# Token rows picked by index: 64 tokens on two partition halves, or 96 tokens on 96 partitions

## What is computed

```python
gate = softmax(top_s)                                   # 8 heads x 16 per token
u = take(expert_u, eidx)                                # row of 1024 for each picked expert
act = gelu(einsum('thkd,td->thk', u, xb))
v = take(expert_v, eidx)
out = einsum('thk,thkd->td', gate * act, v)
```

## Time and profile before

| | us |
|---|---|
| median of 3 runs | 2746.68 (2738.3 to 2747.53) |
| profiled execution, its own time | 2742.25 |
| its span, first to last instruction | 2740.9 |
| TensorE busy | 2560.6 (93%) |
| VectorE busy | 1730.9 (63%) |
| ScalarE busy | 1015.2 (37%) |
| GpSimd busy | 381.0 (14%) |
| matmuls of 448 columns, up and down | 6144 |

### The profile page before, as it was taken

The page is one execution under the profiler, slowest core; times in us unless marked ns, Lnnn a source line. Parts: engine busy times, 40 slices in busy tenths (PEclk is TensorE's granted clock), DMA queues, the critical chain, the costliest instruction groups (busy, mean ns, idle before and its releaser), DMA issues.

```text
span 2740.9 us, 33410 instructions
## 1 busy us (share of the span) xinstructions
PE 2560.6 (93%) x12530; PEld 2093.6 (76%) x12530; DVE 1730.9 (63%) x3522; ACT 1015.2 (37%) x1687; POOL 381.0 (14%) x256
## 2 busy tenths in 40 slices
PE   7989999999999999999999999899877899999997
PEld 5768988988888888999999997678644476645555
DVE  7898867766676665766777645553467645255564
ACT  3332333343333332333333333432256523244443
POOL 4010444440000001212222000200000020000001
PEclk9999999999999999999999999999899999999999
DMA  6546444446566569998999753111100012100001
GB/s 237 181 170 231 144 144 144 144 151 215 199 212 220 200 216 336 317 300 278 317 318 303 242 204 117 56 52 62 38 1 1 1 63 76 64 18 18 18 1 62
DMA packets 148415, 415.91 MB, mean 152 GB/s; under 512 B 13664, under 2 KB 75232, under 8 KB 145568
## 3 DMA queue, kind: packets, MB, share of 16 engines
q1 hardware_dynamic: 100896, 317.31, 33.2%
q0 software_dynamic: 18432, 67.12, 7.4%
q10 hardware_dynamic: 28928, 29.36, 3.4%
HBM read 352.62 MB, written 60.82 MB: 151 GB/s over the span
## 4 chain that ended last, share of the span: by engine, by line
PE 83%; DVE 9%; ACT 4%; issue 4%; POOL 1%; DMA 0%; ACTq 0%; DVEq 0%
PE psum L542 8%; PE psum L543 8%; PE psum L544 8%; PE psum L411 7%; PE psum L413 7%; PE psum L412 7%; PE psum L403 5%; PE psum L405 5%; PE psum L404 5%; PE psum L515 4%; PE psum L827 2%; PE psum L429 2%; DVE small L1669 2%; PE psum L847 2%; PE psum L696 1%
## 5 line engine op out<-in xcount | busy, mean ns | idle before, releaser
L1332 DVE TENSOR_TENSOR weights_low<-arena,weights_high 128x1024 fp32r<-128x1024 f32 x290 | 364.1, 1256 | 517.2 <-ACT weights_high L904 516.6
L904 ACT ACTIVATE weights_high<-arena 128x1024 fp32r<-128x1024 f32 x355 | 374.4, 1055 | 560.5 <-PE psum L544 412.5
L411 PE MATMUL psum<-x_high,weights_high 128*128 128x448 f32 x1024 | 380.4, 371 | 7.6 <-POOL weights_low L1862 7.6
L542 PE MATMUL psum<-hidden_high,weights_high 128*128 128x448 f32 x1024 | 375.9, 367 | 6.8 <-issue 6.8
L543 PE MATMUL psum<-hidden_low,weights_high 128*128 128x448 f32 x1024 | 375.0, 366 | 0.0
L544 PE MATMUL psum<-hidden_high,weights_low 128*128 128x448 f32 x1024 | 375.0, 366 | 0.0
L413 PE MATMUL psum<-x_high,weights_low 128*128 128x448 f32 x1024 | 374.1, 365 | 0.0
L412 PE MATMUL psum<-x_low,weights_high 128*128 128x448 f32 x1024 | 374.0, 365 | 0.0
L403 PE MATMUL psum<-x_high,weights_high 128*128 128x512 f32 (+1 forms) x696 | 277.8, 399 | 24.3 <-DVE weights_low L1332 19.4
L404 PE MATMUL psum<-x_low,weights_high 128*128 128x512 f32 (+1 forms) x696 | 272.6, 392 | 0.0
L405 PE MATMUL psum<-x_high,weights_low 128*128 128x512 f32 (+1 forms) x696 | 272.6, 392 | 0.0
(11 more groups left out here) (239 smaller groups left out, 3976.9 us busy)
## 6 DMA issues: line engine op xcount, KB each, us to landing
arena<-in_stream SPq DMA_DIRECT2D x227, 512.0 KB
arena<-in_v_rows SPq DMA_DIRECT2D x128, 512.0 KB
hidden<-arena SPq DMA_DIRECT2D x128, 224.0 KB, 2.5
router<-arena SPq DMA_DIRECT2D x14, 2048.0 KB, 8.3
arena<-hidden SPq DMA_DIRECT2D x128, 224.0 KB, 4.9
arena<-router ACTq DMA_DIRECT2D x16, 1792.0 KB
arena<-in_ada_w SPq DMA_DIRECT2D x48, 512.0 KB, 3.4
arena<-in_pair_w SPq DMA_DIRECT2D x8, 576.0 KB, 3.8
```

What stands on the lines that cost most here:

```text
L411: PE.matmul(bank[b][:, 0:N], wh[u % 2][:, k, :], xh[:, k, PICKED:T], start=k == 0, stop=False)
L542: PE.matmul(out, wh[w][:, n, :], hh[:, r, :], start=e == 0, stop=False)
L904: ACT.activation(wh[u % 2], slots[u % RING], AF.Copy).then_inc(*tick("weights_high", u))
L1332: DVE.tensor_tensor(wl[u % 2], slots[u % RING], wh[u % 2].bitcast(F32), ALU.subtract).then_inc(*tick("weights", u))
```

## The change

`PICKED` goes from 64 to 96, one token per partition on 96 partitions, all 128 entries of a token there; so N is 416, there are 104 quads and 13 stages, and 256 rows are gathered (128 of each table, 96 partitions each) instead of 128. Rows of both tables come in turn: an `expert_v` row of entry n follows 12 entries behind its `expert_u` row, gelu and the product with the gates are done in groups of 8 entries, and there is one sum. The moves between partitions and `twice` go. VectorE uses one row in each of up steps 6 to 56, two in each of 57 to 63, and 191 rows spread over down steps 0 to 123. `weigh_hidden` goes from VectorE to GpSimd, two steps ahead, in one list with the gathers.

```diff
-PICKED = 64
+PICKED = 96
 N = T - PICKED
-PICKS = PICKED * ENTRIES // P
+GROUP = 8
+ROW_LAG = 12
...
+    ROWS = []
+    for n in range(ENTRIES + ROW_LAG):
+        ROWS += [("u", n)] * (n < ENTRIES) + [("v", n - ROW_LAG)] * (n >= ROW_LAG)
+    ROW_STEPS = [("up", n) for n in range(1, KEYS - UNDER_ROUTER)] + [("down", e) for e in range(KEYS)]
+    ROWS_AT = {step: [] for step in ROW_STEPS}
+    LAST_ROWS = KEYS - 4
+    early = len(range(6, 57)) + 2 * len(range(57, 64))
+    for j in range(early):
+        ROWS_AT["up", 6 + j if j < 51 else 57 + (j - 51) // 2].append(j)
+    for e in range(LAST_ROWS):
+        rest = len(ROWS) - early
+        ROWS_AT["down", e] = list(range(early + e * rest // LAST_ROWS, early + (e + 1) * rest // LAST_ROWS))
...
+        def gelu_rows(step):
+            for g in GELU_AT.get(step, []):
+                part = row_act[:, g * GROUP:(g + 1) * GROUP]
+                ACT.wait_ge(*at("row_used", ROWS.index(("u", (g + 1) * GROUP - 1))))
+                ACT.activation(part, part, AF.Gelu_apprx_tanh).then_inc(*tick("row_act", g))
...
         for e in range(KEYS):
-            if e + 1 < KEYS:
-                weigh_hidden(e + 1)
             low_weights(unit("down", e) + 1)
             if e + 1 < KEYS:
                 hidden_low(e + 1)
-            use_row(("down", e))
...
+            for j in ROWS_AT["down", e]:
+                use_row(j)
...
+        def weigh_hidden(e):
...
+            POOL.wait_ge(*at(f"hidden{e % HID_RING}_in", e))
+            POOL.wait_ge(*at(f"g{e // BLOCK % 2}_in", e // BLOCK))
+            POOL.tensor_tensor(one, one, gates, ALU.mult).then_inc(*tick("weighted", e))
+
+        POOL.wait_ge(*at("chosen", 0))
+        for j in range(ROW_RING):
+            fetch_row(j)
+        for kind, n in ROW_STEPS:
+            if kind == "down":
+                for e in range(2) if n == 0 else ():
+                    weigh_hidden(e)
+                if n + 2 < KEYS:
+                    weigh_hidden(n + 2)
+            for j in ROWS_AT[kind, n]:
+                fetch_row(j + ROW_RING)
...
-        load("x_rows_moved", 0, x_rows[PICKED:P, :], x_rows[0:PICKED, :])
...
-        load("chosen_moved", 0, chosen[PICKED:P, 0:PICKS], chosen[0:PICKED, PICKS:ENTRIES])
-        load("row_gate_moved", 0, row_gate[PICKED:P, :], gate[0:PICKED, 0, PICKS:ENTRIES])
```

More of the change, by code:

```diff
@@ L337, in taken @@
         return "convolved", n - 12
[L340 to L348, removed]
+    ROWS = []
[10 more added lines that the diff above has]
+        ROWS_AT["down", e] = list(range(early + e * rest // LAST_ROWS, early + (e + 1) * rest // LAST_ROWS))
+    GELU_AT = {}
+    for at_step, step in enumerate(ROW_STEPS):
+        for j in ROWS_AT[step]:
+            if ROWS[j][0] == "u" and ROWS[j][1] % GROUP == GROUP - 1:
+                GELU_AT.setdefault(ROW_STEPS[at_step + 1], []).append(ROWS[j][1] // GROUP)
     def a_tiles(t):
@@ L548, in tensor @@
                     if n == 0:
-                        PE.wait_ge(*at("row_acc", "both"))
-                    PE.matmul(bank[n][:, 0:PICKED], row_acc[0][:, n * P:(n + 1) * P], K("twice"), start=True,
-                              stop=True).then_inc(*tick("summed_down", n))
+                        PE.wait_ge(*at("row_used", len(ROWS) - 1))
+                    PE.matmul(bank[n][:, 0:PICKED], row_acc[:, n * P:(n + 1) * P], K("ident", slice(0, PICKED))[:, 0:PICKED],
+                              start=True, stop=True).then_inc(*tick("summed_down", n))
         def embed(n):
@@ L1555, in vector @@
                 one_hots(i)
-            use_row(("up", n))
-        def weigh_hidden(e):
-            one = hidden[:, e % HID_RING, :].rearrange("p (s t) -> p s t", t=STAGE)
-            block = weight[:, e // BLOCK % 2 * STAGES:(e // BLOCK % 2 + 1) * STAGES, :]
-            gates = block.rearrange("p s (e t) -> p s e t", t=STAGE)[:, :, e % BLOCK, :]
-            DVE.wait_ge(*at(f"hidden{e % HID_RING}_in", e))
-            DVE.wait_ge(*at(f"g{e // BLOCK % 2}_in", e // BLOCK))
-            DVE.tensor_tensor(one, one, gates, ALU.mult).then_inc(*tick("weighted", e))
+            for j in ROWS_AT["up", n]:
+                use_row(j)
         def hidden_low(e):
@@ L1863, in gpsimd, with fetch_row @@
                 *tick("weights_pool", u))
[L1865 to L1867 removed]
+        def fetch_row(j):
+            if j >= len(ROWS):
+                return
             if j >= ROW_RING:
                 POOL.wait_ge(*at("row_used", j - ROW_RING))
[L1870 to L1873 removed]
+            table, entry = ROWS[j]
+            POOL.indirect_dma_start(rows[j % ROW_RING], None, d[f"{table}_rows"], bass.IndirectOffsetOnAxis(
+                ap=chosen[:, entry:entry + 1].bitcast(U32), axis=0)).then_inc(*tick(f"row{j % ROW_RING}_in", j, 16))
+        def weigh_hidden(e):
+            one = hidden[:, e % HID_RING, :].rearrange("p (s t) -> p s t", t=STAGE)
+            block = weight[:, e // BLOCK % 2 * STAGES:(e // BLOCK % 2 + 1) * STAGES, :]
+            gates = block.rearrange("p s (e t) -> p s e t", t=STAGE)[:, :, e % BLOCK, :]
+            POOL.wait_ge(*at(f"hidden{e % HID_RING}_in", e))
[12 more added lines that the diff above has]
+                fetch_row(j + ROW_RING)
         for c in range(KC - 1):
```

91 lines of the change are left out of this document (36 added, 55 removed).

## The result

The changed kernel takes 2777.97 us in the median of 4 runs (2775.98 to 2790.25), the kernel before 2747.11 beside it. The ratio is 1.0128, with a 95% interval from 1.0091 to 1.0165 (the quotient of the two medians is 1.0112). The forecast was 2684, its range 2661 to 2723. The profiled execution spans 2775.7 us, 34.8 more than the 2740.9 of before.

What follows compares the result with a forecast made beforehand. TensorE was taken to bound the first up and down stages, a four-engine ring the second up stage. Gains 17 + 11 - 1 + 35.6 = 62.6 us off 2742.25 gave 2679.6, with the median 4.4 above: 2684, range 2661 to 2723.

Steps and rivals of the forecast that it cites:

- Full DMA showed 398, so it fits at 86%: Down stage: 1.56 MB a step in 4.54 us needs 343 GB/s, within the 398 GB/s seen at full DMA.
- Rival 3: Down stage: the ring of four row buffers becomes the bound, 5.39 us a step, total 2785; chance 0.07.
- VectorE beside GpSimd: Down stage: weighing on GpSimd costs VectorE 0.85 us a step through contention, bounds 0.4 to 1.3.
- rival 1: Down stage: VectorE becomes the bound, weighing costs it 1.3 us a step, time about 2713; chance 0.20.
- 4.33 us a step, 95% of TensorE's 4.54: Down stage: VectorE's work of 3.48 us plus 0.85 for contention stays under TensorE's step.
- The first up stage: Beside the expert search: 64 units each 0.32 us shorter, less longer waits once a head; gain 17 us.
- the second: Second up stage: two-quad steps gain nothing, eight one-quad steps gain 1.6 us each, gelu loses 1.5; gain 11 us.
- the ring: Second up stage: scatter, eviction, rounding, subtraction and one-hots through four engines set a two-quad step at 7.32 us.
- Rival 2: All goes well: second up stage's ring gives way (15.4 us more), DMA adds nothing; 87 us gained, 2660; chance 0.11.
- The last seven ups and the change of stage: Between up and down stages: units gain 2.2 us, idle grows from 6.8 to about 10; net loss 1 us.

Runs made afterwards that it cites:

- e2: The changed kernel with gathers fetching rows for all 128 partitions, the last 32 unused: 2730.26 us.
- e3: The changed kernel with PICKED at 64, rows gathered to 64 partitions: 2787.12 us.
- e5: A separate kernel computing nothing, only gathers and loads: beside loads 409 GB/s with 128 partitions, 293 with 96, 260 with 64.
- e1: The changed kernel with the weighing of hidden blocks back on VectorE, 96-partition gathers kept: 2774.85 us.
- e4: The changed kernel with each gather bringing only half a row (2 KB) per partition, the other half zero: 2729.64 us.
- e6: The changed kernel with 128-partition gathers (32 unused) and the weighing back on VectorE: 2684.92 us, ratio 0.9800.
- e10: The kernel before, ScalarE rounding next weights ahead of the quads' evictions in the second up stage: that stage 405.7 to 368.5 us, kernel 1% faster.
- e11: The changed kernel, ScalarE rounding next weights ahead of the quads' evictions in the second up stage: that stage 393.1 to 341.7 us.

## Why the prediction was wrong

**The step that failed is "Full DMA showed 398, so it fits at 86%".** The 398 GB/s came from a stretch of the kernel before in which every transfer went to 128 partitions. The change makes 39% of the bytes gathers to 96 partitions, and with these a full DMA moves 286 GB/s. The same 1.56 MB a step take 1.56 / 0.286 = 5.45 us, 698 us for 128 steps (691 measured), where 4.54 was forecast. e2, e3 and e5 show it, and e1 and e4 fit: more partitions and more bytes are faster, fewer partitions and fewer bytes slower, and it is there with no compute engine at work. The range had no case for it, since I let a ceiling stand for all transfers. Rows 1 held a warning: the down stage's own 275 GB/s at a share of 0.82 are 335 at full share, less than the 343 that I asked of it. That figure would have been wrong as well (e6 moves 380 in this stage), and it would not have been enough: 1.56 MB at 335 GB/s are 4.65 us a step, 14 us more than the forecast and inside its range.

**Rival 3 gave nearly the right time (2785) by a neighbouring mechanism.** Its place and length are right: the down stage, 5.40 us a step for its 5.39 (691.4 us for 128). Its cause, the ring's depth at a DMA share of 86%, is not: the share is 1.03, and a fifth buffer gives back 16 of the 65 us. That the time came out near is luck.

**VectorE beside GpSimd: 0.85 us a step forecast, 0.82 measured (e2 against e6).** The size held, and so did the mechanism, and rival 1 with its 1.3 us fell. The conclusion from it, "4.33 us a step, 95% of TensorE's 4.54" and therefore fitting, failed: in e2 VectorE is busy 517 of 600 us, 4.35 a step, and the step is 5.05 long. A load that fits on average is not a schedule that fits. I counted what VectorE gives up, and left out that GpSimd is stopped in turn: its weighings have a mean of 1.28 us in e2 for 1.11 free, its gathers one of 1.64 (1.08 in the down stage of before). The gathers are as long in e6 (1.63), where they hold nobody up; in e2 they stand in one list with the weighing, for which TensorE's next unit waits. Behind wide gathers or half rows this second limit makes 646 to 651 of the down stage (e2, e4; forecast 591, before 626). Moving the weighing was a loss on its own: under 128-partition gathers it costs 2730 against 2685.

**The first up stage** (17 forecast, 19.8 measured) and **the second** (11 forecast, 12.6) held. e3 confirms the count of steps (112 quads: 405.8), e10 and e11 confirm the ring by cutting it. Rival 2's ring that gives way fell. I had read the ring rightly and not asked what it costs: it was to me a reason why fewer columns gain nothing there, and not 37 us that lie open in the kernel before (e10).

**The last seven ups and the change of stage** were mis-sized: 1 us forecast, 8.1 measured. The cause was right in kind, more rows in a window where DMA is full, and it was divided by 398 GB/s where 323 were moved. The place was wrong: the 6.8 us idle at the change of stage did not become about 10 but 5.52, and the loss lies in the last up units, where ScalarE waits 13.90 us for the store of a hidden block and TensorE then 8.91. The same wait of ScalarE stands in e2 (11.5 us) and in e6 (11.1), not in e4 with half rows, where the same edit gains 3 us; so full DMA makes it with wide gathers too.

With both causes removed the forecast's sum comes out: e6 is at 2684.92, down stage 594.7 for 590.7. That is another kernel than the one forecast (more bytes, the weighing on VectorE), and to 1 us the agreement is luck.

## What to carry to other kernels

A ceiling of GB/s read from a trace holds for the shape of the transfers in it: where an edit changes how many partitions a gather writes, measure that gather beside the loads it will share the engines with. If fewer than 128 partitions are needed, it can be cheaper to bring rows for all 128, or to find work for them. And before an operation moves to an engine whose list also issues gathers, ask what stands behind it when either side waits; busy shares of 86% and 75% on two engines that stop each other were already too much.

## What the runs showed of the hardware

- Full DMA engines moved 409 GB/s with gathers to 128 partitions beside loads, 293 with 96 and 260 with 64; the loads' packets slowed down with the gathers' (163, about 231 and about 256 ns for 4 KB).
- A two-input operation of GpSimd and one of VectorE exclude each other in both directions: 1.21 becomes 2.61 us on VectorE, 1.11 becomes 2.41 on GpSimd (e4). GpSimd's issue of a gather is stretched too: 0.94 us to 128 partitions with VectorE idle (e5, and all 29 from 640 to 1040 in the kernel before), 1.64 in the mean in e2's down stage and 1.63 in e6's, where GpSimd has no other operation; the stretching stands beside VectorE's work and isn't isolated further. The Trainium skill, "SBUF — State Buffer", section Who interferes with whom, calls it an exclusive lock in which the second to issue blocks entirely; the two durations agree with a lock. The row at 1302.17, in which the engine with the earlier record waits, can't test the order, because a gather's issue was still under way on GpSimd. That section of the Trainium skill names only operations of GpSimd that read SBUF against VectorE's two-input ones; the gathers' issue grew here as well.
- The same kernel with 96 tokens swings from 2685 to 2778 us by nothing but the width of its gathers and the engine of one multiplication.
